# Behind the expert block: the projection of the delta gate goes last, and its Silu is taken straight from the projection's result

## The chip, the cores and the metric

The kernel runs on one core of one Trainium2 chip. Its time is the device time of one execution, in microseconds (us). Five engines work side by side, each in the order of its own program: TensorE (PE in the profile, with PEld for its weight loads), VectorE (DVE), ScalarE (ACT), GpSimd (POOL) and SyncE (SP), which here issues all the transfers. They wait for each other through semaphores.

## The reference, cut to what matters

Two blocks of a transformer follow each other over 256 tokens of width 1024. The first holds neighbourhood attention, a gated recurrence and 16 experts. The second begins with a hybrid mixer. Its input projection is one matrix, whose columns are cut into several parts:

```python
qkv = jax.nn.silu(depthwise_conv_centred(p[..., :OFF_Z_A], conv_w))          # 1536 columns
za = p[..., OFF_Z_A:OFF_BA_A].reshape(bsz, n_tok, A_HEADS, A_HEAD_DIM)       # 512 columns: "z"
ba = p[..., OFF_BA_A:OFF_Q_B]                                                # 16 columns
qb = rms_norm_2(p[..., OFF_Q_B:OFF_K_B].reshape(...), q_norm)                # 512 columns: "q"
kb = rms_norm_2(p[..., OFF_K_B:OFF_V_B].reshape(...), k_norm)                # 128 columns
vb = p[..., OFF_V_B:].reshape(bsz, n_tok, B_KV_HEADS, B_HEAD_DIM)            # 128 columns
...
y = rms_norm_2(o, out_norm) * jax.nn.silu(z.astype(F32))                     # delta_readout
```

The gated delta rule takes qkv and ba. Grouped-query attention takes qb, kb and vb, after an axial rotation of qb and kb. The gate z is wanted much later: it multiplies the delta rule's output when that is complete.

## The kernel before, in words

Everything is float32, and tokens lie in two tiles of 128 (t = 0, 1). Each engine has one long program, written out by hand. Loops on different engines meet only at semaphores, so the order in which a program is written is the order of work.

Weights pass through a ring of six slots in SBUF. SP issues the transfers in a fixed order, and each waits until the weights six places ahead in the order have been used. Matmul results go to eight PSUM banks, six of which rotate here. `bank_filled` says that a result is complete, `bank_drained` that it has been read.

The stretch behind the experts, in the order of TensorE's program:

- the twelve feature blocks of qkv ("qkv", line 1284), each passed through a short convolution on VectorE (L2415, L2419), a Silu on ScalarE (L3068) and a transpose on TensorE (L446, a helper that makes all 128x128 transposes);
- `project("hyb", "z", ...)` and then `project("hyb", "q", ...)`, 512 columns each for both token tiles. Their matmuls are recorded at L555;
- "bkv": the 16 columns of ba with grouped keys and values, 272 columns (L1308);
- transposes of the grouped queries ("qbT") once VectorE has given `grouped_query_ready`, and of the grouped keys ("kbT") once it has given `grouped_key_ready`. ScalarE copies them out (L3086, L3091);
- grouped attention: 16 steps (two token tiles, eight heads). A step has the scores (L1332), one eighth of a modulation product, which is independent work (L467), the transposes of the exponentials of two steps before (L446), and the product with the values of three steps before (L1345). The first three steps have scores and modulation only; then come the first transposes, the fourth step's scores and modulation, the second transposes, and with them the first values.

VectorE in the same stretch: it normalises the heads of qkv (L2176 to L2185), copies z out of PSUM (L2433), copies q out (L2438), takes q's mean squares, scales, rotates and scales again (L2444 to L2459, both tiles, which ends in `grouped_query_ready`), copies bkv out (L2463), and does the same for the keys (L2196 to L2475, which ends in `grouped_key_ready`). ScalarE takes the three square roots in it (L2690). The Silu of z runs on ScalarE behind the attention (L3100), in place, and `delta_gate` tells VectorE's readout of the delta rule, long after.

The first block's neighbourhood attention has the same form in its own lines: scores at L753 and L755, modulation at L467, transposes at L446, values at L768.

## Time and profile before

| | |
|---|---|
| time before, median of 3 runs | 2674.57 us (2674.56 to 2683.15) |
| span of the profiled execution | 2689.2 us |
| TensorE busy | 2163.9 us, 80% of the span |
| VectorE, ScalarE, GpSimd busy | 599.4, 343.5, 97.0 us |
| chain that ended last | TensorE 54%, transfers 40%, VectorE 3%, ScalarE 2% |

The profiled execution is one more execution of the same program, and the profile gives only its span. Line numbers (L555) are lines of the kernel before. A row of a timeline gives the start in us from the span's start, the time from the first to the last of the merged instructions, and what they are. In square brackets stands how long the engine was idle ahead of them and what released it. TensorE makes two records of one float32 matmul, so the counts in the trace are twice those of the program's order.

### The profile page before, as it was taken

To read this page: it belongs to the slowest core of one execution; us is meant where nothing else is said; L and a number is where in the kernel's file an instruction comes from. 1 tells how busy PE (TensorE), PEld (TensorE's weight loads), DVE (VectorE), ACT (ScalarE), POOL (GpSimd) and SP (SyncE) were. 2 spreads that over 40 slices of the span, in tenths; PEclk is the share of its full clock that TensorE was granted. 3 is DMA by queue.
4 is the path that set the end of the run, shared out by engine and by line. 5 is a ranking of instruction groups with operands and counts; after the bars stand their busy time and mean duration, and the time that the engine had idled before them with its cause. 6 is when DMAs were issued, how large, how long until landed. Compare 5 with 4: busy or idle time off the path is not lost.

```text
span 2689.2 us, 35584 instructions
## 1 busy us (share of the span) xinstructions
PE 2163.9 (80%) x15740; PEld 1251.1 (47%) x15740; DVE 599.4 (22%) x1143; ACT 343.5 (13%) x692; POOL 97.0 (4%) x116
## 2 busy tenths in 40 slices
PE   5999998555566565666988865587999999999999
PEld 2444574222223232233554432263576885666874
DVE  1112554001011010112322210055434000461000
ACT  2101222000010000011110100031251000132000
POOL 0001000000000000000111100000030000100000
PEclk8999998999999999999999999988899999999999
DMA  8633706999999999999999999953732454323450
GB/s 329 260 127 140 236 10 230 421 425 425 424 424 422 421 425 415 421 407 424 424 424 424 425 424 425 421 185 105 240 127 63 139 178 153 110 79 113 148 204 37
DMA packets 158907, 755.20 MB, mean 281 GB/s; under 512 B 12249, under 2 KB 75737, under 8 KB 102050
## 3 DMA queue, kind: packets, MB, share of 16 engines
q1 hardware_dynamic: 158754, 752.92, 70.6%
q8 instruction: 125, 2.05, 0.3%
q14 instruction: 28, 0.23, 0.0%
HBM read 751.83 MB, written 1.05 MB: 280 GB/s over the span
## 4 chain that ended last, share of the span: by engine, by line
PE 54%; DMA 40%; DVE 3%; ACT 2%; issue 1%; POOL 0%; DVEq 0%; SPq 0%; ACTq 0%; POOLq 0%
DMA ring<-w_up_dram 16%; PE psum L653 11%; DMA ring<-w_gate_dram 11%; DMA ring<-w_down_dram 8%; PE psum L555 8%; PE psum L681 5%; DMA ring<-hyb_w_dram 4%; PE psum L1176 3%; PE psum L467 2%; PE psum L1560 2%; PE psum L1240 2%; PE psum L446 2%; PE psum L1284 2%; PE psum L1382 1%; PE psum L1655 1%; PE psum L1015 1%
## 5 line engine op out<-in xcount | busy, mean ns | idle before, releaser
L1176 PE MATMUL psum<-ring,arena 128*32 128x320 f32 x4096 | 360.4, 469 | 281.0 <-DMA ring<-w_gate_dram 141.9
L1176 PEld LDWEIGHTS psum<-ring,arena 128*32 128x32 f32 x4096 | 112.0, 111 | 440.6 <-DMA ring<-w_up_dram 170.8
L653 PE MATMUL psum<-arena,ring 128*128 128x256 f32 x1408 | 305.5, 380 | 0.0
L1240 PE MATMUL psum<-ring,arena 128*32 128x512 f32 x1344 | 212.0, 606 | 107.3 <-DMA ring<-w_down_dram 107.3
L653 PEld LDWEIGHTS psum<-arena,ring 128*128 128x128 f32 x1408 | 268.5, 191 | 36.6
L555 PE MATMUL psum<-ring,arena 128*128 128x512 f32 x480 | 213.3, 606 | 10.3 <-ACT arena L2760 8.5
L1240 PEld LDWEIGHTS psum<-ring,arena 128*32 128x32 f32 x1344 | 47.4, 109 | 247.2 <-DMA ring<-w_down_dram 171.8
L555 PEld LDWEIGHTS psum<-ring,arena 128*128 128x128 f32 x480 | 92.7, 195 | 128.2 <-issue 128.2
L2337 DVE TENSOR_TENSOR arena<-arena,psum 128x320 f32<-128x320 f32 (+1 forms) x32 | 16.7, 521 | 580.5 <-PE psum L1176 574.6
L681 PE MATMUL psum<-ring,arena 128*128 128x512 f32 x288 | 125.0, 596 | 0.0
L1185 PE MATMUL psum<-ring,arena 128*32 128x64 f32 x2048 | 119.8, 291 | 0.0
L1185 PEld LDWEIGHTS psum<-ring,arena 128*32 128x32 f32 x2048 | 69.1, 111 | 84.1 <-issue 79.0
L446 PE MATMUL psum<-consts,arena 128*128 128x128 f32 x470 | 80.3, 309 | 30.8 <-DVE arena L1737 8.7
L467 PE MATMUL psum<-ring,cols 128*32 128x512 f32 x576 | 88.2, 717 | 18.1 <-DMA ring<-w_mod_dram 18.1
L446 PEld LDWEIGHTS psum<-consts,arena 128*128 128x128 f32 x470 | 62.9, 167 | 82.6 <-issue 54.0
L681 PEld LDWEIGHTS psum<-ring,arena 128*128 128x128 f32 x288 | 55.2, 192 | 68.6 <-issue 68.5
L1893 DVE TENSOR_TENSOR arena<-arena,psum 128x512 f32<-128x512 f32 x22 | 15.1, 687 | 290.3 <-PE psum L653 290.3
L1069 PE MATMUL psum<-arena 128*128 128x128 f32 x544 | 73.6, 284 | 1.3
L1069 PEld LDWEIGHTS psum<-arena 128*128 128x128 f32 x544 | 64.9, 193 | 16.6 <-issue 16.6
L3034 ACT COPY arena<-psum 128x512 f32<-128x512 f32 x32 | 18.8, 586 | 407.5 <-PE psum L1240 407.5
L3021 ACT ACTIVATE arena<-psum 128x320 f32<-128x320 f32 (+1 forms) x32 | 14.9, 465 | 376.7 <-PE psum L1176 372.7
L986 PE MATMUL psum<-arena 128*128 128x512 f32 x128 | 59.2, 605 | 0.8 <-issue 0.8
(376 smaller groups left out, 2121.0 us busy)
## 6 DMA issues: line engine op xcount, KB each, us to landing
ring<-w_gate_dram SPq DMA_DIRECT2D x128, 1376.0 KB, 18.1
ring<-w_up_dram SPq DMA_DIRECT2D x128, 1376.0 KB, 18.1
ring<-w_down_dram SPq DMA_DIRECT2D x112, 1536.0 KB, 19.9
ring<-w_mod_dram SPq DMA_DIRECT2D x72, 1024.0 KB, 5.1
ring<-w_ffn_in_dram SPq DMA_DIRECT2D x88, 512.0 KB, 5.1
ring<-w_ffn_out_dram SPq DMA_DIRECT2D x14, 1536.0 KB, 7.4
ring<-w_in_dram SPq DMA_DIRECT2D x16, 1024.0 KB, 5.6
ring<-hyb_w_dram SPq DMA_DIRECT2D x10, 1024.0 KB, 16.8
```

Of the source, the lines that this page charges most:

```text
L446: return nc.tensor.transpose(o, i, const("ident")[0:i.shape[0], 0:i.shape[0]])
L467: ins = nc.tensor.matmul(psum[32 * j:32 * j + 32, bank, :], stat, w[:, j, :], start=(k == 0), stop=(k == KT - 1), skip_group_check=True)
L555: ins = nc.tensor.matmul(banks[t][:, 0:n], XTt(kk, t), w[:, k, :], start=(kk == 0), stop=(kk == 7), skip_group_check=True)
L653: ins = nc.tensor.matmul(b[:, i * 256:(i + 1) * 256], ws[k // 4][:, k % 4, u, i * P:(i + 1) * P], R(XT + k * 256, 256), start=(k == 0), st ...
L681: ins = nc.tensor.matmul(banks[2 * t + c], R(HTF + k * 256 + t * P, P), w[:, (k % 3) * D + c * HALF:(k % 3) * D + (c + 1) * HALF], start=( ...
L986: ins = nc.tensor.matmul(b, R(SALL + e * 256 + t * P, P), R(YS + c * HALF, HALF), start=True, stop=True, skip_group_check=True)
L1069: ins = nc.tensor.matmul(result(tag)[:, h * P:(h + 1) * P], lhs(h), rhs(h), start=True, stop=True, skip_group_check=True)
L1176: ins = nc.tensor.matmul(banks[u][c][32 * j:32 * j + 32, 0:GMAIN], R(XST + k * HALF + e * CAP, CAP), w3[:, 64 * c:64 * c + 64, QGROUP * j: ...
L1185: ins = nc.tensor.matmul(banks[u][1][32 * j:32 * j + 32, GMAIN:GMAIN + GEXTRA], R(XST + k * HALF + e * CAP, CAP), extra, start=False, stop ...
L1240: ins = nc.tensor.matmul(ybanks[half][32 * c:32 * c + 32, :], stationary, w, start=((half, c) not in begun), stop=(unit >= 36), skip_group ...
L1284: ins = nc.tensor.matmul(b[:, 0:SEQ], w[:, k, f * P:(f + 1) * P], R(XT + k * 256, SEQ), start=(k == 0), stop=(k == 7), skip_group_check=True)
L1560: ins = nc.tensor.matmul(b[:, i * 256:(i + 1) * 256], ws[k // 4][:, k % 4, u, i * P:(i + 1) * P], R(XT + k * 256, 256), start=(k == 0), st ...
```

## The change

Grouped queries are projected first, then grouped keys and values, and the gate block z last. The three weight loads change places in the same way. VectorE no longer copies z out; ScalarE applies the Silu to z straight from PSUM, between its third square root and its copies of the transposed queries, with a load of the Silu table ahead of it. The two Silu instructions behind the attention and the semaphore `delta_gate` go, and the readout waits for the drained bank instead.

```diff
@@ TensorE
-            project("hyb", "z", range(2), 512)
             project("hyb", "q", range(2), 512)
             enlist(("hyb", "bkv"))
...
                     if t == 1 and k == 7:
                         frees(("hyb", "bkv"), ("bkv", t))
+            project("hyb", "z", range(2), 512)

             pe.wait_ge(grouped_query_ready, tally.due(grouped_query_ready, 2))
@@ VectorE
             unit_heads(tmp, [R(at + t * HALF, HALF) for at in (QL, KL) for t in range(TT)], 16, unit_qk_ready)
-            for t in range(TT):
-                v.wait_ge(bank_filled[bank_of(("hyb", "z", t))], nth(("hyb", "z", t)))
-                ins = v.tensor_copy(R(ZG + t * HALF, HALF), result(("hyb", "z", t)))
-                ins.then_inc(bank_drained[bank_of(("hyb", "z", t))], 1)
-                v.wait_ge(bank_drained[bank_of(("hyb", "z", t))], nth(("hyb", "z", t)))
...
             readout("dlo", [R(E0 + t * HALF, HALF) for t in range(TT)], row("out_norm"),
-                    lambda t: v.wait_ge(delta_gate, tally.due(delta_gate)),
+                    lambda t: v.wait_ge(bank_drained[bank_of(("hyb", "z", t))], nth(("hyb", "z", t))),
@@ ScalarE
             root(sm(592, 4))
+            a.preload_act_table(ACT.Silu)
+            for t in range(TT):
+                tag = ("hyb", "z", t)
+                a.wait_ge(bank_filled[bank_of(tag)], nth(tag))
+                ins = a.activation(R(ZG + t * HALF, HALF), result(tag), ACT.Silu)
+                ins.then_inc(bank_drained[bank_of(tag)], 1)
             for t in range(TT):
                 dst = R(QBT, 1024).rearrange("p (i n) -> p i n", i=4)[:, :, t * P:(t + 1) * P]
...
             betas(0)
-            for t in range(TT):
-                z = R(ZG + t * HALF, HALF)
-                a.activation(z, z, ACT.Silu).then_inc(delta_gate, 1)
-                a.wait_ge(delta_gate, tally.gave(delta_gate))
             gate_decays(0, "gsums", "gsums1")
@@ SyncE
-            proj_in("hyb", T["hyb_w"], 1536, 512, "z")
+            proj_in("hyb", T["hyb_w"], 2064, 512, "q")

             s.wait_ge(x_ready, tally.due(x_ready, 4))
             post_rows(T["g_mix_post"][0], T["g_ffn_post"][0], (WP2, WT2))
-            proj_in("hyb", T["hyb_w"], 2064, 512, "q")
             grouped_in(("hyb", "bkv"))
+            proj_in("hyb", T["hyb_w"], 1536, 512, "z")
```

The order of TensorE's instructions from the last feature block of qkv to the first scores, before: z and q are the first and the second half of the 32 matmuls at L555.

```order
L1284 MATMUL psum<-arena,ring 128x256 x8
L446 MATMUL psum<-consts,arena 128x128 x6
L555 MATMUL psum<-ring,arena 128x512 x32
L1308 MATMUL psum<-ring,arena 128x272 x16
L446 MATMUL psum<-consts,arena 128x128 x16
L1332 MATMUL psum<-arena 128x512
```

The same place in the changed kernel, whose lines lie one or two lower: q is the first row of 16 at L554, z the second.

```order
L1283 MATMUL psum<-arena,ring 128x256 x8
L445 MATMUL psum<-consts,arena 128x128 x6
L554 MATMUL psum<-ring,arena 128x512 x16
L1306 MATMUL psum<-ring,arena 128x272 x16
L554 MATMUL psum<-ring,arena 128x512 x16
L445 MATMUL psum<-consts,arena 128x128 x16
L1331 MATMUL psum<-arena 128x512
```

The 16 matmuls of z have moved from ahead of q to between bkv and the 16 transposes.

ScalarE's order from the last transposes of qkv to the first exponentials of the attention, before:

```order
L3077 COPY arena<-psum 128x2x128 x2
L2690 ACT_TABLE_LOAD
L2690 ACTIVATE small<-small 128x16 x2
L2690 ACTIVATE small<-small 128x4
L3086 COPY arena<-psum 128x4x128 x2
L3091 COPY arena<-psum 128x512 x2
L2956 ACT_TABLE_LOAD
```

And in the changed kernel, with the table load at L3077 and the Silu of z at L3081:

```order
L3071 COPY arena<-psum 128x2x128 x2
L2684 ACT_TABLE_LOAD
L2684 ACTIVATE small<-small 128x16 x2
L2684 ACTIVATE small<-small 128x4
L3077 ACT_TABLE_LOAD
L3081 ACTIVATE arena<-psum 128x512 x2
L3086 COPY arena<-psum 128x4x128 x2
L3091 COPY arena<-psum 128x512 x2
L2950 ACT_TABLE_LOAD
```

The load and the two Silu instructions now stand between the last square root and the first copy of transposed queries. The number of table loads in the program is the same, since the one ahead of the old Silu (L3100) is gone.

## Rows read from the trace of the kernel before

**Rows 1.** The page: its first line.

```profile
span 2689.2 us, 35584 instructions
```

**Rows 2.** TensorE's timeline from the projections to the first scores.

```profile
1823.43 27.63 PE L555 MATMUL psum<-ring,arena 128*128 128x512 f32 x64
1850.90 7.50 PE L1308 MATMUL psum<-ring,arena 128*128 128x272 f32 x32
1864.24 1.97 PE L446 MATMUL psum<-consts,arena 128*128 128x128 f32 x8 [5.85 <-DVE arena L2459]
1872.22 1.97 PE L446 MATMUL psum<-consts,arena 128*128 128x128 f32 x8 [6.01 <-DVE arena L2475]
1875.12 2.04 PE L1332 MATMUL psum<-arena 64*128 64x512 f32 x2 [0.93 <-ACT arena L3091]
```

**Rows 3.** VectorE's timeline of the same stretch.

```profile
1837.43 0.69 DVE L2433 COPY arena<-psum 128x512 f32<-128x512 f32 x1 [2.74 <-PE psum L555]
...
1851.17 0.69 DVE L2438 COPY arena<-psum 128x512 f32<-128x512 f32 x1 [2.74 <-PE psum L555]
...
1863.76 0.43 DVE L2459 TENSOR_SCALAR arena<-arena 128x512 f32<-128x512 f32 x1
...
1871.22 0.95 DVE L2475 COPY arena<-arena 128x256 f32<-128x256 f32 x3
```

**Rows 4.** ScalarE's timeline of the same stretch.

```profile
1866.73 0.20 ACT L2690 ACTIVATE small<-small 128x4 f32<-128x4 f32 x1 [11.46 <-DVE small L1721]
...
1874.28 0.59 ACT L3091 COPY arena<-psum 128x512 f32<-128x512 f32 x1 [0.27 <-PE psum L446]
...
1881.04 0.69 ACT L2776 ACTIVATE arena<-psum,small 128x512 f32<-128x512 f32 x1
```

**Rows 5.** ScalarE's groups in the feed-forward: Silu from PSUM (xcount, busy us, mean ns).

```profile
L2789 ACT ACTIVATE arena<-psum 128x512 f32<-128x512 f32 x11 | 6.6, 598 | 137.4 <-PE psum L653 137.4
```

**Rows 6.** Issues of hyb_w on SyncE's queue, and one's landing (KB, us).

```profile
1736.33 25.62 SPq L3406 DMA_DIRECT2D ring<-hyb_w_dram  x6
...
1786.56 23.04 SPq L3406 DMA_DIRECT2D ring<-hyb_w_dram  x4
...
ring<-hyb_w_dram SPq DMA_DIRECT2D x1, 1024.0 KB, 5.0
```

**Rows 7.** Chain that ended last, in the attention: start, us, what.

```profile
1881.03 1.86 PE psum L467 x8
...
1886.76 1.05 PE psum L446 x4
...
1896.34 0.84 PE psum L1345 x8
1897.17 1.05 PE psum L1332 x2
...
1900.65 1.05 PE psum L1332 x2
```

**Rows 8.** TensorE by stretches: us, busy, granted clock, share of DMA, GB/s.

```profile
262.80:265.00 2.20, 2.19 (x13) 0.94 0.03 7
265.00:278.40 13.40, 13.40 (x44) 0.50 0.70 235
...
1858.40:1862.00 3.60, 0.00 (x0) 1.00 0.74 228
1862.00:1875.10 13.10, 3.94 (x16) 0.51 0.04 18
1875.10:1892.50 17.40, 17.38 (x48) 0.50 0.54 182
```

**Rows 9.** TensorE's timeline into the first block's neighbourhood attention.

```profile
256.73 3.66 PE L446 MATMUL psum<-consts,arena 128*128 128x128 f32 x32
262.81 0.67 PE L753 MATMUL psum<-arena 64*128 64x256 f32 x2 [2.43 <-ACT arena L2843]
...
278.42 1.00 PE L768 MATMUL psum<-arena 128*128 128x64 f32 x8
```

**Rows 10.** VectorE's timeline behind the attention.

```profile
1943.84 1.29 DVE L1967 COPY arena<-psum 128x512 f32<-128x512 f32 x2 [3.95 <-PE psum L446]
```

More of the change, by code:

```diff
@@ L225, in program @@
         softplus_log = semaphore("softplus_log")
-        delta_gate = semaphore("delta_gate")
         conf_mean_in = semaphore("conf_mean_in")
```

## The prediction

> **What bounds the kernel now.** I began with the page's first line [rows 1], which gives the execution against which all sums are made, and went then to the stretch that the change touches, engine by engine. TensorE's timeline is the one to start with, since TensorE or what it waits for carries the end. The two projections run without a gap from 1823.43 and the keys' and values' projection follows them at once until 1850.90 + 7.50 = 1858.40 [rows 2]. Then TensorE stands still twice: 5.85 us for L2459, the last step of the grouped queries, and 6.01 us for L2475, the last step of the grouped keys. After a third wait of 0.93 us, for ScalarE's copies, the first scores start at 1875.12. Between the end of the projections and the first scores lie 16.72 us, with only 16 transposes in them.
>
> The reader should then look at VectorE, which both waits name. Its chain begins when the second tile of q is complete, with the copy at 1851.17, and goes on almost without idling to the end of the queries' work at 1863.76 + 0.43 = 1864.19 and of the keys' at 1871.22 + 0.95 = 1872.17 [rows 3]. So VectorE needs 13.0 us from that copy for the queries and 21.0 us for both. It was free long before: it waited 2.74 us for L555, that is for TensorE to finish q. What bounds this stretch is how early q is complete.
>
> The last view is the granted clock. It is 1.00 (2.4 GHz) until 1862, four microseconds into the first wait, and 0.50 (1.2 GHz) from there to the start of the values at about 1892.5, although TensorE is busy for 17.38 of the last 17.40 us [rows 8]. The wait is therefore paid a second time, in the first steps of the attention.
>
> **Part one: q ahead of z.** The amount of TensorE's work is the same, so the three projections end at 1858.40 as before. Now q comes first. The second copy of z, which stood at the end of the first projection, started at 1837.43 [rows 3]. The second copy of q starts there now. It stood at 1851.17, so VectorE's chain moves by 13.74 us. Nothing ahead of it holds it back, since VectorE waited 2.74 us for TensorE even there. The queries are ready at 1864.19 - 13.74 = 1850.45, and the keys at 1872.17 - 13.74 = 1858.43. The copies of bkv inside the chain, now at about 1850.5, find it complete at 1837.2 + 7.5 = 1844.7. The last square root, ScalarE's at 1866.73 [rows 4], comes at 1853.0, and it stands ahead of the Silu of z in ScalarE's order, so it does not wait for z.
>
> TensorE therefore comes out of z at 1858.40 and finds the queries ready since 8 us. The eight transposes of queries take about 0.9 us, since 32 such took 3.66 us at the full clock [rows 9], or 0.114 us each. The keys' turn comes at 1859.3, after their 1858.43. Both waits on VectorE go to nothing, with a margin of 8 us for the first and 0.9 us for the second. All 16 transposes end near 1860.2.
>
> **Part two: the Silu of z on ScalarE.** The operation itself, Silu from PSUM on 128x512, is in the trace at 598 ns [rows 5]. The first tile is complete at about 1855 and its Silu lies beside TensorE's work. The second is complete with TensorE's last z matmul, so it runs from about 1858.7 (the copies of rows 3 started 0.27 us behind the end of the matmuls) to 1859.3. Queued behind it are the four copies of queries and keys, for which the first scores wait. Their first input is complete at about 1859.1, so the Silu delays them by 0.2 us. Four copies of 0.59 us [rows 4] end at 1861.7, and 0.25 us later, as before (1875.12 behind 1874.28 + 0.59), the scores start, at 1861.9. The table load ahead of the Silu comes at about 1853.3, when ScalarE has nothing else to do until 1855. If that cover were gone it would cost its own length. Behind the attention, ScalarE loses two Silus and a load, but there VectorE waits 3.95 us for TensorE's transposes and not for ScalarE [rows 10], so I count nothing. The two copies of z that VectorE loses lay in its waits for TensorE, so they count nothing either.
>
> The sum of parts one and two is 1875.12 - 1861.9 = 13.2 us.
>
> **Part three: the weights.** In SyncE's order q takes z's place, so its transfers go out with the six issues from 1736.33, which are over by 1762, and it is wanted at 1823. The four issues from 1786.56 to 1809.6 were q's two and bkv's two; now they are bkv's two and z's two. With 5.0 us from issue to landing [rows 6] the last is in by 1815, and z is wanted at 1844.7. The modulation weights behind them wait for slots that come free at the same times as before, because the ring counts places and the sizes of work between are the same. Cost nothing, cover 30 us.
>
> **Part four: the clock.** The attention's steps are priced at both levels by rows 7. At 0.50 the modulation takes 1.86 us and four transposes 1.05; at 1.00 the scores take 1.05 and a whole step from one L1332 to the next 1900.65 - 1897.17 = 3.48. Before, everything ahead of the values ran at 0.50: 17.4 us. What it does now is the one thing that this trace does not show for this place, so I bound it. At the lower end the clock is at half for the whole of it, and nothing is gained. At the upper end it stays at full: scores and modulation take 1.05 + 1.86 / 2 = 2.0 us a step, three steps end at 1867.9, and the transposes then wait for ScalarE's first exponential. That started 1881.04 - 1874.87 = 6.17 us behind the last key copy and took 0.69 [rows 4], so it now ends near 1868.6. TensorE starts 0.25 us later, and with transposes at half of 1.05, another step and transposes again (0.5 + 2.0 + 0.5) the values start at 1871.9, where before they started at 1892.5. That is a gain of 20.6 us in all, 7.4 of them from the clock.
>
> Between the two ends there is a near relative of this place in the same trace. The neighbourhood attention also comes behind dense projections and a train of transposes, then waits 2.43 us for ScalarE's copies, and starts with scores on 64 rows and modulation [rows 9]. The wait here will be 1.7 us. There the clock was 0.94 in the mean over the first 2.2 us and then 0.50 for 13.4 us, in which TensorE was busy all the time, and full again as the values began [rows 8]. Its way from first scores to first values was 278.42 - 262.81 = 15.6 us, against 17.4 us here. I take that value, the nearest row: 1.8 us gained, to be added to 13.2, so 15.0 us.
>
> The Trainium skill, in "TensorE: Matmul & The Clock Gate", Part 1, says that "activity releases the throttle", so that a busy array has the full clock again soon. By that rule the half clock of a busy stretch would be short, and the sum would be the upper end. Rows 8 speak against it, with 13.4 us and 17.4 us at 0.50 and full busy time. Part 4 of the same page says that transposes don't count as TensorE's work in the same way; with the projections' end as the last real work, that would favour the fall that rows 8 and 9 show.
>
> **The rivals.** *The clock stays up* (chance 0.27): the wait is shorter than in the relative, 1.7 against 2.43 us, and transposes end closer to it. The values then start at 1871.9, the gain is 20.6 us and the time 2654.0 us. Against it stands the relative, which fell.
>
> *The clock comes back late* (0.16): the clock is half from the first scores on, as before, and comes back not with the first values but some 3 us into them. Each microsecond at half does half the work, so this costs 1.6 us of the 13.2. The gain is 11.6 us and the time 2663.0 us. For it speaks that the two returns seen came within half a microsecond of the first values and need not again; against it, that it happened twice.
>
> *The waits only move* (0.05): if ScalarE's queue or the keys' chain is later than I think, the scores wait again. The margin of the keys is 0.9 us, every microsecond beyond it costs one, and 12 us would have to be found to bring the gain near nothing. I see no such row. The time would be 2672 us or so.
>
> *It becomes slower* (0.04): the attention is entered at half clock and stays there. A step at half takes twice the scores, 1.86 us of modulation, 1.05 of transposes and twice 0.84 of values, together 6.7 us against 3.48 [rows 7], 3.2 us more. Beyond 13.2 / 3.2 = four such steps with values in them the change loses, and eight and a half cost another 0.5%. Against it: in both attentions the clock came back with the first values.
>
> **How the numbers follow.** My forecast (0.48) is 15.0 us less. Against the profiled span that is 2689.2 - 15.0 = 2674.2 us. The median of the runs lies 14.6 us under that span; the stretch I changed waits for no transfer, so I take the same difference from the median: 2674.6 - 15.0 = 2659.6 us. With the next two cases the sum of chances is 0.91, from 2654.0 to 2663.0, and I give 3 us on both sides for runs that differ and for where clock changes fall behind the attention: 2651 to 2666. Half a per cent, 13.4 us, is about what a measurement of this kernel can tell from no change, and lies only 1.6 us below the forecast, so I let a quarter of the first case fall short of it: faster is three quarters of 0.48, the 0.27 of the second case and a little of the third, 0.66; slower 0.04; the rest, 0.30, is the same.
>
> **What would show it.** Right: TensorE goes from z into transposes with no wait for VectorE. The wait ahead of the first scores is under 2 us, for ScalarE's key copies. The first scores come 13 us earlier against the start of the projections (38.5 us behind it instead of 51.7). The first values come 53 to 55 us behind the start of the projections if the clock falls, 49 if it holds, and 69 before. Wrong: a wait for VectorE ahead of the keys' transposes of more than 1 us, a wait for hyb_w at the z projection, or a granted clock at half in the steps with values.

## The result

Five executions of the changed kernel have a median of 2652.93 us (2646.3 to 2668.32); five of the kernel before, on the same chip and in the same call, 2683.15 us (2674.56 to 2696.42). The ratio is 0.9894 [0.9862, 0.9926], so the change makes the kernel 1.1% faster. A second measurement of the same code gave 0.9886 [0.9866, 0.9905]. The 72 executions of the kernel before that ran beside the other kernels have a mean of 2686.0 us, the 11 of the changed kernel one of 2657.3 us: 28.7 us less, give or take about 4.5. (The 2674.57 us of the first table, a median of three, lies 11.4 us below that mean.) Left out of means and ratios are two executions of the kernel before at over 3000 us and one of `filler`, further down, at 2720.61 us.

TensorE's timeline of the changed kernel, from the last transposes of qkv into the attention, in the columns of [rows 2]. Lines lie one or two lower than before.

```profile
1813.69 0.44 PE L445 MATMUL psum<-consts,arena 128*128 128x128 f32 x2 [2.15 <-ACT arena L3062]
1813.97 15.60 PE L554 MATMUL psum<-ring,arena 128*128 128x512 f32 x32
1829.40 7.50 PE L1306 MATMUL psum<-ring,arena 128*128 128x272 f32 x32
1836.73 13.90 PE L554 MATMUL psum<-ring,arena 128*128 128x512 f32 x32
1850.47 1.91 PE L445 MATMUL psum<-consts,arena 128*128 128x128 f32 x16
1853.85 1.09 PE L1331 MATMUL psum<-arena 64*128 64x512 f32 x2 [1.47 <-ACT arena L3091]
1854.87 1.06 PE L466 MATMUL psum<-ring,cols 128*32 128x512 f32 x8
...
1860.60 0.66 PE L445 MATMUL psum<-consts,arena 128*128 128x128 f32 x4 [0.57 <-ACT arena L2770]
...
1863.73 1.00 PE L1344 MATMUL psum<-arena 128*128 128x64 f32 x8
```

The two waits for VectorE of [rows 2] are gone, and all 16 transposes are one group of 1.91 us. Scores take 1.09 us and modulation 1.06 us from the first step on; in the kernel before they took 2.04 and 1.86. The first scores start 39.88 us behind the projections' start (51.69 before), the first values 49.76 us behind it (69.08 before).

VectorE's timeline of the changed kernel, which answers to [rows 3]:

```profile
1829.67 0.69 DVE L2432 COPY arena<-psum 128x512 f32<-128x512 f32 x1 [2.74 <-PE psum L554]
...
1842.27 0.43 DVE L2453 TENSOR_SCALAR arena<-arena 128x512 f32<-128x512 f32 x1
...
1849.72 0.95 DVE L2469 COPY arena<-arena 128x256 f32<-128x256 f32 x3
```

ScalarE's timeline of the changed kernel, which answers to [rows 4]:

```profile
1845.23 0.20 ACT L2684 ACTIVATE small<-small 128x4 f32<-128x4 f32 x1 [11.46 <-DVE small L1720]
1845.46 1.28 ACT L3077 ACT_TABLE_LOAD   x1
1847.23 0.60 ACT L3081 ACTIVATE arena<-psum 128x512 f32<-128x512 f32 x1 [0.49 <-PE psum L554]
1850.67 0.60 ACT L3081 ACTIVATE arena<-psum 128x512 f32<-128x512 f32 x1 [2.84 <-PE psum L554]
1851.16 1.20 ACT L3086 COPY arena<-psum 128x512 f32<-128x512 f32 x2
1852.39 1.20 ACT L3091 COPY arena<-psum 128x512 f32<-128x512 f32 x2
...
1859.77 0.69 ACT L2770 ACTIVATE arena<-psum,small 128x512 f32<-128x512 f32 x1
```

The keys are ready at 1849.72 + 0.95 = 1850.67, the queries 8 us before, and TensorE goes from z into the transposes at 1850.47. What TensorE still waits for is ScalarE's four copies.

TensorE by stretches in the changed kernel, with the columns of [rows 8] (behind PE's busy time those of PEld, DVE, ACT and POOL, then the granted clock):

```profile
1813.00:1829.00 16.00, 15.30 (x34) 6.77 (x35) 9.70 (x17) 2.66 (x5) 0.00 (x0) 0.89 0.28 101
1829.00:1850.00 21.00, 21.00 (x65) 12.13 (x64) 18.15 (x43) 2.30 (x4) 0.00 (x0) 1.00 0.44 150
1850.00:1862.00 12.00, 9.96 (x54) 3.88 (x52) 4.71 (x15) 9.27 (x16) 0.00 (x0) 1.00 0.69 237
1862.00:1875.00 13.00, 13.00 (x87) 6.93 (x86) 5.48 (x9) 3.06 (x9) 0.00 (x0) 1.00 0.96 352
```

The clock is 1.00, so 2.4 GHz, from the transposes through the first steps of the attention, where [rows 8] have 0.50. It is below 1.00 only at the start of the projections, behind the 2.15 us wait: 0.89 over 16 us, which is some 3.5 us at half. Therefore q took 15.60 us and not 13.9.

**Where the time went.** Five marks on TensorE's timeline divide an execution: A, the first matmul of qkv (L1283 or L1284); B, the start of the projections; C, the first scores; D, the first values; E, the first sum of the gates behind the attention (L1053 or L1054); F, the first matmul of the next feed-forward (L652 or L653). All in us, from one profiled execution each.

| profile | A at | B to C | C to D | D to E | A to E | E to F | F to end | span |
|---|---|---|---|---|---|---|---|---|
| before | 1775.19 | 51.69 | 17.39 | 46.42 | 163.74 | 139.28 | 611.0 | 2689.2 |
| before_again | 1776.63 | 51.71 | 17.39 | 46.58 | 164.27 | 145.49 | 608.4 | 2694.8 |
| after | 1765.87 | 39.88 | 9.88 | 46.23 | 144.09 | 135.30 | 605.8 | 2651.1 |
| after_again | 1766.05 | 38.19 | 9.88 | 46.24 | 142.63 | 133.53 | 610.6 | 2652.8 |

In the changed stretch, A to E, the two pairs differ by 164.0 - 143.4 = 20.6 us. The profiled executions differ by 40 us, because those of before also came to A 10.0 us later, and took 9.5 us longer from E on. Ahead of A the change only has another block of hyb_w loaded, and behind E only the Silu of z is gone (two of 0.63 us and a load). Behind that Silu ScalarE still waited 1.03 us for TensorE in the kernel before, so it was not in the way. Of the 28.7 us between the many executions this stretch accounts for 20.6 us, and some 8 us are to be sought elsewhere.

### The profile page after: what moved, and what is told of

Its sections match the earlier page's. It is cut to its first block and busy times, and to the rows that moved or that the text cites. A ratio compares the mean times of both kernels' runs of the same rounds, so it can differ in the third digit from the quotient of the medians.

```text
span 2651.1 us, 35579 instructions
## 1 busy us (share of the span) xinstructions
PE 2132.5 (80%) x15740; PEld 1235.2 (47%) x15740; DVE 598.3 (23%) x1141; ACT 343.1 (13%) x692; POOL 97.3 (4%) x116
## 5 line engine op out<-in xcount | busy, mean ns | idle before, releaser
L652 PE MATMUL psum<-arena,ring 128*128 128x256 f32 x1408 | 306.4, 381 | 0.0
L652 PEld LDWEIGHTS psum<-arena,ring 128*128 128x128 f32 x1408 | 269.1, 191 | 36.9
L554 PE MATMUL psum<-ring,arena 128*128 128x512 f32 x480 | 215.6, 610 | 10.4 <-ACT arena L2754 8.6
L554 PEld LDWEIGHTS psum<-ring,arena 128*128 128x128 f32 x480 | 93.5, 196 | 129.6 <-issue 129.5
L2336 DVE TENSOR_TENSOR arena<-arena,psum 128x320 f32<-128x320 f32 (+1 forms) x32 | 16.7, 521 | 580.6 <-PE psum L1175 574.6
L466 PE MATMUL psum<-ring,cols 128*32 128x512 f32 x576 | 79.9, 656 | 18.3 <-DMA ring<-w_mod_dram 18.3
L445 PE MATMUL psum<-consts,arena 128*128 128x128 f32 x470 | 74.9, 293 | 19.2 <-DVE arena L1736 8.3
## 6 DMA issues: line engine op xcount, KB each, us to landing
ring<-hyb_w_dram SPq DMA_DIRECT2D x10, 1024.0 KB, 16.7
```

What stands on the lines that cost most here:

```text
L445: return nc.tensor.transpose(o, i, const("ident")[0:i.shape[0], 0:i.shape[0]])
L466: ins = nc.tensor.matmul(psum[32 * j:32 * j + 32, bank, :], stat, w[:, j, :], start=(k == 0), stop=(k == KT - 1), skip_group_check=True)
L554: ins = nc.tensor.matmul(banks[t][:, 0:n], XTt(kk, t), w[:, k, :], start=(kk == 0), stop=(kk == 7), skip_group_check=True)
L652: ins = nc.tensor.matmul(b[:, i * 256:(i + 1) * 256], ws[k // 4][:, k % 4, u, i * P:(i + 1) * P], R(XT + k * 256, 256), start=(k == 0), st ...
```

## The experiments

My theory behind the first result was that two effects add up: the chain on VectorE starts earlier, some 13 us, and TensorE's waits ahead of the attention no longer cost it the clock, 7.4 us. The rivals were that the Silu's place has a part in it, that the clock falls or holds by the position in time and not by the waits, and that the gain beyond 20.6 us belongs to the new order too. Twelve kernels ran: two repeat the two kernels, three do or undo one part, five put idle or busy time at one place, and two go beyond the change. Each ratio is to the kernel before on the same chip.

### The two kernels again

`after_again` and `before_again` are the two kernels without an edit.

> The changed kernel once more, with a profile of its own, to part what the change does from what differs between executions. In the first profiles the span fell by 38.1 us, of which 19.3 lie between the start of the projections (1823.43 before, 1813.97 after) and the end of the attention, 9.5 ahead of it and 9.3 behind it. Theory: only the 19 us belong to the change; the other 19 are chance, so this profile's stretch from the end of the attention to the end of the span lies anywhere between the two seen (750.3 and 741.0 us), and the ratio is near 0.993 (19 of 2680). Rival: the change also shortens what follows, then the stretch behind the attention is again 741 us within 2 and the ratio near 0.989.

Measured: 2658.2 us, ratio 0.9886 [0.9866, 0.9905]. Here the clock did not fall at the start of q:

```profile
1814.10 0.44 PE L445 MATMUL psum<-consts,arena 128*128 128x128 f32 x2 [2.15 <-ACT arena L3062]
1814.37 13.90 PE L554 MATMUL psum<-ring,arena 128*128 128x512 f32 x32
...
1852.56 1.09 PE L1331 MATMUL psum<-arena 64*128 64x512 f32 x2 [1.47 <-ACT arena L3091]
```

q takes 13.90 us, and the first scores come 38.19 us behind the projections' start. The 1.7 us by which the first profile was later are the half clock at the start of q, and nothing else. Before the run I had taken only 19 us for the change's own, with a ratio near 0.993; the rival there, that the gain goes on behind the attention, asked for a ratio near 0.989 and for 741 us from E to the end within 2. The ratio came as the rival had it, and the stretch from E on took 744.1 us, between the two. So 0.9894 was not a chance of the first measurement.

> The kernel before once more, for a second profile. The first block, which no variant touches, took 9.4 us longer up to the feature blocks of qkv in the two profiles with z first (before, and the Silu alone) than in the four with q first, and the difference lies in the neighbourhood attention, where the clock fell in the two and not in the four. Theory: that is chance, decided by some tenths of a microsecond of where TensorE stands when the clock is reviewed, so it may come out either way here; the stretch from the projections to the end of the attention is 115.5 us again. Rival (something in the changed program keeps the clock up in the first block): the feature blocks start at 1775 again. Ratio 1.000.

Measured: 2686.2 us, ratio 1.000 [0.9975, 1.0026]. A difference under 0.3% is not to be told from none. A came at 1776.63, and the clock fell in the first block's attention again: the sign that I had named for the rival, that something in the changed program keeps the clock up there. Later runs speak against its plain form, since that clock also fell in `gap12` and `covered_one_table`, which have the new order, and held in `filler6`, which has the old one.

### The order alone, and the Silu alone

`order_only` has the changed order on TensorE and SyncE. VectorE copies z behind the keys, and ScalarE does the Silu behind the attention as before. Against the changed kernel:

```diff
@@ VectorE, ahead of log_decays(0)
+            for t in range(TT):
+                v.wait_ge(bank_filled[bank_of(("hyb", "z", t))], nth(("hyb", "z", t)))
+                ins = v.tensor_copy(R(ZG + t * HALF, HALF), result(("hyb", "z", t)))
...
@@ ScalarE
-            a.preload_act_table(ACT.Silu)
-            for t in range(TT):
...
-                ins = a.activation(R(ZG + t * HALF, HALF), result(tag), ACT.Silu)
...
             betas(0)
+            for t in range(TT):
+                z = R(ZG + t * HALF, HALF)
+                a.activation(z, z, ACT.Silu).then_inc(delta_gate, 1)
```

> The three projections and their weights in the changed order, but the gate handled as before: VectorE copies z out (now behind the keys, ahead of the log decays), ScalarE takes the Silu behind the attention. Theory (the order is the cause): no wait of TensorE for VectorE ahead of the transposes, the first scores about 39 us behind the start of the projections, as in the changed kernel (39.9). The two z copies of 0.69 us then stand ahead of the soft plus and so of the first exponential, which comes 1 to 1.5 us later; the time is within 3 us of the changed kernel's. Rival (the gain lies in taking the Silu at once): the time is near that of before.

Measured: 2663.8 us, ratio 0.9903 [0.9879, 0.9927]. The median is 5.6 us above that of `after_again`, measured beside it, where I had expected 3 at most, but the intervals overlap. The first exponential did not come later either: it starts 5.92 us behind the first scores in both. In the stretch it is the same within 0.02 us: B to C 39.90 and C to D 9.88. The order carries the gain of the stretch.

`silu_only` keeps z first and gives ScalarE the Silu from PSUM, with a load of the square root's table behind it. VectorE's two copies and the Silu behind the attention go, as in the changed kernel:

```diff
@@ ScalarE, against the kernel before
             root(sm(576, 16))
+            a.preload_act_table(ACT.Silu)
+            for t in range(TT):
+                tag = ("hyb", "z", t)
+                a.wait_ge(bank_filled[bank_of(tag)], nth(tag))
+                ins = a.activation(R(ZG + t * HALF, HALF), result(tag), ACT.Silu)
+                ins.then_inc(bank_drained[bank_of(tag)], 1)
+            a.preload_act_table(ACT.Sqrt)
             root(sm(576, 16))
             root(sm(592, 4))
```

> The projections and weights in the order of before (z, q, keys and values), but ScalarE takes the Silu of z straight from PSUM, between its first square root and the second, with loads of the Silu and the square-root table around it; VectorE's two copies and the Silu behind the attention are gone. Theory: nothing on the path changes, TensorE waits 5.9 and 6.0 us for VectorE as before, the first scores come 51.7 us behind the start of the projections, and the ratio is 1.000 within the noise. Rival (the Silu is the gain): most of the 19 us between the projections and the attention's end appear here.

Measured: 2683.5 us, ratio 0.9987 [0.9963, 1.001]. TensorE's waits stand as in [rows 2]:

```profile
1864.49 1.97 PE L445 MATMUL psum<-consts,arena 128*128 128x128 f32 x8 [5.79 <-DVE arena L2453]
1872.48 1.97 PE L445 MATMUL psum<-consts,arena 128*128 128x128 f32 x8 [6.02 <-DVE arena L2469]
```

Where the Silu stands is worth nothing by itself. In the changed kernel it only must not be in the way of the copies, and it is not: with it the scores come 1853.85 - 1850.47 = 3.38 us behind the start of the transposes, in order_only, without it, 1853.77 - 1850.37 = 3.40.

### Keys and values last

`bkv_last` has the order q, z, bkv on TensorE and SyncE:

```diff
@@ TensorE and SyncE, against the changed kernel
             project("hyb", "q", range(2), 512)
+            project("hyb", "z", range(2), 512)
             enlist(("hyb", "bkv"))
...
-            project("hyb", "z", range(2), 512)
```

> As the changed kernel, but z between q and the keys' and values' projection, which comes last. Theory: the queries' work is hidden, the keys' is not, since VectorE can only begin it with bkv complete. TensorE waits about 7.4 us for VectorE ahead of the keys' transposes (8.0 us of key work behind the end of the projections, less the queries' transposes), and the first scores come near 46 us behind the start of the projections instead of 39.9. Whether the clock falls in that wait is open: 6 us slower than the changed kernel if it holds, 13 if it falls. Rival (it is enough that q comes first): no wait there, and the changed kernel's time.

Measured: 2678.9 us, ratio 0.9967 [0.9948, 0.9986].

```profile
1850.47 1.04 PE L445 MATMUL psum<-consts,arena 128*128 128x128 f32 x8
1858.28 1.97 PE L445 MATMUL psum<-consts,arena 128*128 128x128 f32 x8 [6.77 <-DVE arena L2469]
1861.21 2.04 PE L1331 MATMUL psum<-arena 64*128 64x512 f32 x2 [0.96 <-ACT arena L3091]
```

The same kernel by stretches, from the last 1.9 us of that wait to the values:

```profile
1856.40:1878.60 22.20, 19.36 (x56) 5.99 (x57) 6.50 (x19) 7.87 (x14) 0.00 (x0) 0.50 0.42 142
```

The queries are ready as in the changed kernel, the keys are not: one wait of 6.77 us stays. From its last 1.9 us on the clock is half for 22 us, and C to D takes 17.39 us as before. So one of the two waits was enough to lose the clock. The median is 20.7 us above that of `after_again`, where I had expected 13; 16 of these lie in A to E.

### Busy work in the waits, in the old order

`filler` and `filler6` are the kernel before with matmuls whose result nobody reads, 12 (6) ahead of each of the two waits for VectorE:

```diff
@@ TensorE, against the kernel before
+            for i in range(6):
+                nc.tensor.matmul(psum[:, 6, :], const("ident"), R(XT, HALF), start=True, stop=True, skip_group_check=True)
             pe.wait_ge(grouped_query_ready, tally.due(grouped_query_ready, 2))
```

> The kernel before, with 12 idle matmuls (128x128 by 512 columns, results never read) in each of the two waits for VectorE, so that TensorE works through both at its full clock. 12 of 0.43 us fill 5.2 of 5.9 and of 6.0 us. Theory (the second half of the gain is the clock): the first scores come 51.7 us behind the start of the projections as before, but the first values about 10 us behind the first scores instead of 17.4, and the whole is 7.5 us faster than before. Rival (the half clock belongs to the attention's first steps, whatever comes ahead): 17.4 us again and the time of before, or worse.

Measured: 2675.3 us, ratio 0.9966 [0.994, 0.9991]. I had sized the filling wrongly: such a matmul takes 0.87 us, so 12 of them took 10.46 us and pushed the scores back by 6.7 us. Still the clock held and C to D took 9.89 us. In the stretch 6.7 us were lost and 7.5 won, so the ratio's 9 us are for the most part not from there.

> The kernel before with six more 128x128x512 matmuls, whose results nobody reads, in each of TensorE's two waits for VectorE (5.85 and 6.01 us); everything else as before. By the trace of the first such kernel one of these takes 0.87 us, so six take 5.2 us and fit into each wait. If idleness of TensorE ahead of the attention is what brings the clock down: the first scores come at 51.7 us behind the start of the projections as before, the clock stays at full, and the first values come some 10 us behind the scores instead of 17.4, at 61.6. That would be 7.4 us in the stretch, and a ratio of 0.995 to 0.998 to the kernel before. If transposes are what lets the clock go, whatever stands in the waits: values at 69 as before, ratio 1.000.

Measured: 2673.8 us, ratio 0.9949 [0.9931, 0.9967].

```profile
1852.86 5.31 PE L1316 MATMUL psum<-arena,consts 128*128 128x512 f32 x12
1858.88 1.09 PE L446 MATMUL psum<-consts,arena 128*128 128x128 f32 x8 [0.70 <-DVE arena L2463]
1859.80 5.32 PE L1323 MATMUL psum<-arena,consts 128*128 128x512 f32 x12
1866.86 1.09 PE L446 MATMUL psum<-consts,arena 128*128 128x128 f32 x8 [1.74 <-DVE arena L2479]
1869.06 1.09 PE L1336 MATMUL psum<-arena 64*128 64x512 f32 x2 [1.11 <-ACT arena L3095]
```

And by stretches, over the first steps of the attention:

```profile
1869.00:1879.00 10.00, 9.36 (x49) 2.77 (x50) 4.16 (x9) 6.45 (x11) 0.00 (x0) 1.00 0.68 229
```

Here the chain on VectorE is as late as in the kernel before, and the scores start 51.00 us behind B. But the clock is 1.00 over the first steps, and the values come 9.89 us behind the scores and not 17.39. So it was TensorE's idleness that took the clock, and the two effects stand apart: of the 20.6 us some 13 were the late chain and 7.5 the clock. The second part can be had in the old order too, with work that computes nothing: A to E takes 155.32 us, 8.7 less than the mean of the two profiles of before.

### Idle time ahead of the scores, in the new order

`gap2` and `gap12` are the changed kernel with 2 (12) more copies on ScalarE ahead of the key copies, for which TensorE waits. They change no result.

```diff
@@ ScalarE, against the changed kernel
+            for i in range(2):
+                a.copy(diagonals[:, :], consts[:, 0:TT * P]).then_inc(scalar_done, 1)
+                a.wait_ge(scalar_done, tally.gave(scalar_done))
             for g in range(2):
                 a.wait_ge(bank_filled[bank_of(("kbT", g))], nth(("kbT", g)))
```

> The changed kernel with two idle copies (128x256, about 0.37 us each) on ScalarE between its copies of the queries and of the keys, so that TensorE waits about 2.2 us ahead of the first scores instead of 1.5. That is the wait of the first block's attention (2.4 us), from which I forecast a fall of the clock. If the clock falls there: first values about 56 us behind the start of the projections, 6 us slower than the changed kernel. If it holds: 50.5 us and 0.7 us slower.

Measured: 2665.2 us, ratio 0.9919 [0.989, 0.9949].

```profile
1851.65 1.09 PE L1331 MATMUL psum<-arena 64*128 64x512 f32 x2 [2.34 <-ACT arena L3094]
1852.67 1.91 PE L466 MATMUL psum<-ring,cols 128*32 128x512 f32 x8
```

By stretches, from the first scores on:

```profile
1851.60:1855.00 3.40, 3.35 (x11) 0.96 (x12) 0.28 (x2) 2.81 (x4) 0.00 (x0) 0.67 0.03 10
1855.00:1865.50 10.50, 10.50 (x36) 2.35 (x36) 3.88 (x8) 3.62 (x7) 0.00 (x0) 0.62 0.81 263
```

In this one profile a wait of 2.34 us instead of 1.47 goes with just the picture that I had forecast for the changed kernel: the first scores run at full clock, the modulation behind them at half, and C to D takes 14.07 us, 4.2 more for 0.87 us of wait.

> As the last, with twelve such copies: a wait of about 6 us. Theory: the clock falls in it, as in the waits of before, and comes back with the values: first scores 44.5 us behind the start of the projections, first values 62, and 12 us slower than the changed kernel, where the wait alone is 4.5. Rival (only the length of the wait counts): 4.5 us slower.

Measured: 2674.6 us, ratio 0.996 [0.994, 0.9979].

```profile
1866.64 2.04 PE L1331 MATMUL psum<-arena 64*128 64x512 f32 x2 [6.71 <-ACT arena L3094]
```

```profile
1866.60:1879.30 12.70, 12.65 (x35) 2.93 (x36) 2.78 (x7) 5.65 (x9) 0.00 (x0) 0.51 0.50 166
```

With 6.71 us the clock is half from the first scores on, and C to D takes 15.08 us. The wait itself is 5.2 us longer than in the changed kernel and the clock adds as much again. The first values come 58.50 us behind B and not 62, since in this profile q ran at full clock and the clock was back one step ahead of the values.

### Two more matmuls ahead of the transposes

`shift2` puts two matmuls that nobody reads behind z, so that the scores start later without any idleness.

```diff
@@ TensorE, against the changed kernel
             project("hyb", "z", range(2), 512)
+            for i in range(2):
+                nc.tensor.matmul(psum[:, 6, :], const("ident"), R(XT, HALF), start=True, stop=True, skip_group_check=True)
```

> The changed kernel with two more 128x128x512 matmuls, whose results nobody reads, between the projection of z and the transposes: 1.74 us of busy TensorE, no idleness. First scores about 41.6 us behind the start of the projections (38.2 to 39.9 in the two profiles of the changed kernel, plus 1.74), first values 9.9 us behind the scores. If the theory holds that it is the order (TensorE's idleness ahead of the scores) that keeps the clock, not the tenth of a microsecond at which the scores start, the clock stays at full here too. If the position decides, it falls at the scores and the values come 13 to 17 us behind them. From the attention's end to the feed-forward part some 135 us if the 10.2 us of half clock there belong to the old order, 140 if they belong to a position.

Measured: 2666.1 us, ratio 0.9918 [0.9893, 0.9944]. B to C 41.54 us, C to D 9.89: the clock held at this position too. From E to F 135.98 us, which by my expectation meant that the half clock there belongs to the old order. The rows say otherwise. The first two rows are TensorE behind E in this kernel, by stretches, and then the same in the kernel before:

```profile
1917.00:1929.00 12.00, 11.11 (x122) 10.55 (x123) 5.69 (x9) 2.67 (x5) 2.10 (x2) 0.57 0.01 2
```

```profile
1938.90:1950.90 12.00, 11.10 (x124) 10.54 (x125) 6.05 (x9) 4.78 (x8) 2.10 (x2) 0.57 0.00 1
```

and in the changed kernel:

```profile
1909.90:1921.90 12.00, 9.80 (x198) 8.98 (x199) 7.79 (x12) 3.41 (x6) 3.30 (x3) 1.00 0.01 2
```

Half clock behind the attention, 0.57 in the mean of 12 us, is thus not a matter of the old order. It comes in the new order as well, with the attention's start 1.7 us further from B.

### Beyond the change

`covered` takes up what the first profile showed, the waits of 0.75 and 2.15 us ahead of q. The first half of q goes ahead of the last two groups of transposes, which wait for ScalarE.

```diff
@@ TensorE, against the changed kernel
-            for ff in (10, 11):
-                pe.wait_ge(short_conv_ready, tally.due(short_conv_ready))
-                transpose4(("qkvT", ff), [R(COUT + ff % 2 * HALF + t * P, P) for t in range(TT)])
-            project("hyb", "q", range(2), 512)
+            def last_transposes():
+                for ff in (10, 11):
+                    pe.wait_ge(short_conv_ready, tally.due(short_conv_ready))
+                    transpose4(("qkvT", ff), [R(COUT + ff % 2 * HALF + t * P, P) for t in range(TT)])
+            project("hyb", "q", range(2), 512, last_transposes)
```

> The changed kernel with the first half of the q projection ahead of the last two transposes of qkv, for which TensorE waits 0.75 and 2.15 us on ScalarE in the changed kernel; the second half stands behind them. If that wait is on the path, the way from the first qkv matmul to the first scores, 88.0 us in the changed kernel's profile, shortens by 2.9 us to 85.1; if the waiting is also what dropped the clock 1.4 us behind the start of q, by up to 1.6 us more, to 83.5. Ratio to the kernel before some 0.988. If VectorE's chain is held by something else ahead (log decays, its own backlog), nothing: 88.0.

Measured: 2657.6 us, ratio 0.9889 [0.9865, 0.9913].

```profile
1810.96 7.03 PE L554 MATMUL psum<-ring,arena 128*128 128x512 f32 x16
1817.83 0.60 PE L445 MATMUL psum<-consts,arena 128*128 128x128 f32 x4
1818.26 7.03 PE L554 MATMUL psum<-ring,arena 128*128 128x512 f32 x16
...
1849.58 1.09 PE L1334 MATMUL psum<-arena 64*128 64x512 f32 x2 [1.47 <-ACT arena L3094]
```

Both waits are gone and q runs at full clock. From A to C it takes 44.28 + 38.62 = 82.90 us, where the changed kernel took 87.98 and, at full clock, 86.51. The theory of the path was right, 0.6 us more than it asked for. Yet the median is that of the changed kernel: A to E is 3.6 and 5.1 us shorter than in the two profiles of the changed kernel, at most 0.2% of 2657, and the interval is 0.5% wide.

`covered_one_table` adds a named table set with both Exp and Ln ahead of the softplus, and puts the first part of the modulation ahead of the first scores.

```diff
@@ ScalarE and TensorE, against covered
+            a.preload_act_table_set("natural_log_exp_and_others")
             softplus(0)
             attention("gq", WP2)
...
+            modulation_part("mod2_1", 0, 0, 4)
...
-            attention("gq", 16, scores2, values2, lambda i: modulation_part("mod2_1", i // KT, i % KT, 4 + i // KT))
+            attention("gq", 16, scores2, values2,
+                      lambda i: i < 15 and modulation_part("mod2_1", (i + 1) // KT, (i + 1) % KT, 4 + (i + 1) // KT))
```

> As the kernel before it in this list, and two more edits ahead of the attention: ScalarE's softplus (Exp, then Ln) takes the one table set that has both functions, named by hand, so that one load of 1.28 us stands there instead of three; and the first part of the modulation goes ahead of the first scores, into TensorE's wait of 1.5 us for ScalarE's copies. If the loads are on ScalarE's path to the first exponential: it starts 2.6 us earlier against the first scores' release, and TensorE's wait for it behind the scores (0.57 us in the changed kernel) goes; with the modulation part (0.93 us) moved into the wait, the way from the first qkv matmul to the first values is 1.5 us shorter than in the kernel before it in this list. If not, under 0.5 us.

Measured: 2655.6 us, ratio 0.9881 [0.9852, 0.9909]. ScalarE's timeline, with one load where three stood:

```profile
1856.36 1.21 ACT L3096 COPY arena<-psum 128x512 f32<-128x512 f32 x2
1857.59 1.28 ACT L3098 ACT_TABLE_LOAD   x1
1858.88 0.22 ACT L2955 ACTIVATE small<-small 128x16 f32<-128x16 f32 x1
1859.47 0.21 ACT L2958 ACTIVATE small<-small 128x16 f32<-128x16 f32 x1 [0.37 <-DVE small L2230]
1861.19 0.69 ACT L2775 ACTIVATE arena<-psum,small 128x512 f32<-128x512 f32 x1 [1.50 <-DVE small L1854]
```

The first exponential starts 1861.19 - 1857.82 = 3.37 us behind the first scores, in the changed kernel 1859.77 - 1853.85 = 5.92: 2.55 us earlier, as expected. It now waits 1.50 us for VectorE's row maxima (L1854). For TensorE that was worth its wait of 0.57 us, which is gone. The values come at 44.43 + 47.86 = 92.29 us behind A, in covered at 92.80: 0.5 us earlier and not 1.5. The rest comes at the end of the attention, which lacks the moved part: A to E is 137.52 against 139.03 us. It has the shortest stretch and the lowest median of the twelve experiments, but no interval parts it from the changed kernel.

The Trainium skill says in "ScalarE: Activation LUTs", section "Table sets: the hidden batching unit", that one set holds exp and ln, so that both cost one load. The trace agrees. The page gives about 2.7 us for a load, the drain included; here each load instruction took 1.28 us.

## Why the prediction came out as it did

The forecast was 2659.6 us and 15.0 us of gain, with a range of 2651 to 2666; the median was 2652.9 us. The time lay in the range and the direction was right. The case that I called the likeliest is not what happened. What happened is the first rival, "the clock stays up", to which I gave 0.27.

That the time fell into the range is in part luck. The forecast stood on a base of 2674.6 us, a median of three executions, and the mean of 72 is 2686.0, 11.4 us more. In gain I was off by almost a factor of two: 15.0 us were forecast, and 28.7 us lie between the means, 30.2 between the medians. That mean less 15.0 us would have been 2671.0 us, above the range. The rival's 2654.0 us is as lucky: its gain of 20.6 us is the stretch's, 8.1 us short of the whole, and the low base hides that.

**Part one, q ahead of z, was right.** VectorE's chain was to move by 13.74 us against the projections. The second copy of q stood 1851.17 - 1823.43 = 27.74 us behind B and now stands 1829.67 - 1813.97 = 15.70 us behind it, 12.04 us less, and the difference of 1.7 us is the half clock at the start of q, which the repetition did not have. Both waits for VectorE vanished, the keys' with a margin of 0.7 us where 0.9 was worked out (ready at 1850.67, wanted 0.9 us behind 1850.47). First scores 38.5 us behind B were forecast; 39.88 and 38.19 were measured. The sum of parts one and two, 13.2 us, came out at 11.8 and 13.5.

**Part two, the Silu, was right.** It was to cost 0.2 us and cost 0.0 (3.38 us from the first transposes to the scores, against 3.40 in order_only). The wait left over for ScalarE was to be 1.7 us and was 1.47. silu_only shows the other half, that moving the Silu alone brings nothing to be measured.

**Part three, the weights, was right.** No wait for hyb_w stands at any projection of the changed kernel. SyncE's timeline has its last four issues done at 1777.11 + 22.41 = 1799.5. The five such transfers of 1024 KB issued between 1700 and 1830 took 5.5 us in the median from issue to landing, where 5.0 was assumed from one. Even with the 16.7 us of all ten in the program z is there at 1816, and it is wanted at 1836.73:

```profile
1726.74 25.90 SPq L3402 DMA_DIRECT2D ring<-hyb_w_dram  x6
...
1777.11 22.41 SPq L3402 DMA_DIRECT2D ring<-hyb_w_dram  x4
```

**Part four, the clock, is the step that failed.** I wrote: "I take that value, the nearest row: 1.8 us gained", from the first block's attention, where the clock fell behind a wait of 2.43 us. The bound that I had set beside it, values 49 us behind B if the clock holds, was measured at 49.76 and 48.07, and C to D at 9.88 us where 1871.9 - 1861.9 = 10.0 was worked out. With the full clock the stretch's gain was to be 20.6 us; it was 19.65 and 21.1 (A to E, 163.74 - 144.09, and 163.74 - 142.63). So the rival's gain in the stretch was sized to within a microsecond, and it was ranked wrongly.

Two things were wrong with the nearest row. First, the wait there was longer, 2.43 us against 1.7 forecast and 1.47 measured. Behind waits of 1.42 to 1.49 us the clock held in five of five profiles, and in gap2, with 0.87 us more, it fell. That is what one would see if the length of the wait decides, but it is not shown: gap2 is one profile. Second, I took one execution of the relative for its behaviour. All 14 profiles of this study have the same code there and the same wait of 2.39 to 2.43 us. The rows are TensorE's timeline into that attention in the changed kernel, as in [rows 9]:

```profile
263.38 0.67 PE L752 MATMUL psum<-arena 64*128 64x256 f32 x2 [2.40 <-ACT arena L2837]
...
272.64 1.00 PE L767 MATMUL psum<-arena 128*128 128x64 f32 x8
```

Here the clock held, and the values come 9.26 us behind the scores, not 15.61. Of the 14 profiles eight have 9.3 us, five have 15.6 and one has 17.2. The row that I used was one of two outcomes of a wait of 2.4 us, and the rarer one. With that known, the upper end would have been the better forecast.

**What the sum lacked.** The stretch gives 20.6 us and the executions differ by 28.7, give or take 4.5. Two things could fill the rest, and neither is settled. The start: up to A, the profiles of before are 9.1 to 10.8 us later than those of the changed kernel. In the first block's attention the clock costs 6.3 us in one of them and 8.0 in the other. With the new order A came at 1763 to 1767 in order_only, bkv_last, gap2 and covered, and at 1775 in gap12 and covered_one_table, in which the clock fell there; in shift2 it did not fall there, and A came at 1772. If that is chance alone, it cancels in the mean. But it fell in four of the five profiles with the old order and in two of the nine with the new, so that it is chance alone is not shown either.

Behind the attention: E to F takes 139.28, 145.49 and 135.31 us in the three profiles whose waits stand as before (the third is silu_only), mean 140.0, and 129.3 to 139.7, mean 134.7, in the other eleven. These some 5 us have the right size. The traces show what they are: the granted clock, in the mean from E to F, was 0.92, 0.88 and 0.95 in the three profiles and 0.94 to 0.99 in the eleven, and over all 14 the stretch is in the main the longer the lower that mean is (129.29, 132.25 and 134.03 us at 0.99, 145.49 at 0.88). It is not only the fall at E. shift2 and silu_only have that one too, with 135.98 and 135.31 us; before_again has another, 0.85 in the mean of the 69 us that begin 60 us behind E. And over the eleven kernels with an edit, the gain by the ratio less the gain in A to E is between -0.3 and +7.9 us, with a mean of 5. So something of about 5 us comes with nearly every edit. The Silu at E is not it: order_only keeps it there and has 135.10 us. Why the clock falls more often behind the attention in the kernel before, and whether the starts differ in the mean, stays open. No run here parts them.

**The rules of the chip.** The Trainium skill says in "TensorE: Matmul & The Clock Gate", Part 1, that activity releases the throttle. By that rule alone I would have taken the upper end, the 20.6 us that the stretch gave. Rows 8 spoke against the rule and still do: in gap12 TensorE is busy for 12.65 of 12.70 us at 0.51, in bkv_last 19.36 of 22.20 us at 0.50. What decided here was not how soon the clock comes back but that it did not fall ahead of the scores, and the same part says that idleness lets it fall. The runs agree with that: with the waits filled it held, in the old order too.

## What to carry to other kernels

A wait on TensorE can have two prices, its own length and the half clock behind it, and here the second was 7.5 us behind 12 us of waits; so read the granted clock in the stretch behind each wait, and ask of an edit not only how much it shortens the wait but also what the clock does behind what is left of it. A clock effect seen once in a trace is one draw: look for the same code in all profiles at hand before it is taken as the rule of the place. When independent projections follow one another, the one whose result has the longest way through the other engines goes first, and all whose results are waited for go ahead of the one that nobody waits for; getting one of two right (q, z, bkv) brought 9 us where both brought 29.

## What the runs showed of the hardware that I had not expected

- The same instructions behind the same wait of 2.4 us ran at full clock in 8 of 14 profiles and at half in 6. It held where the scores started at 263.29 to 264.05 us, and fell at 261.89 to 263.15, but also once at 263.51, while it held in gap2 at 263.50. The position goes with the outcome but does not settle it.
- A busy TensorE stayed at 1.2 GHz for 12 to 17 us in the first steps of the attention (busy 12.65 of 12.70 us at 0.51 in gap12, 17.38 of 17.40 at 0.50 in the kernel before). In the grouped attention it was back at 2.4 GHz before the first values or less than 2 us behind them, in every profile in which it had fallen.
- The clock fell at the start of the dense q projection, behind a wait of 2.15 us, in the profiles of the changed kernel, order_only, bkv_last, gap2 and shift2, and not in those of after_again and gap12. It cost 1.7 us. With z first it did not fall in five profiles, with the wait covered in none of two. Why it falls there only with q first is not known.
- A 128x128x512 matmul of the filling took 0.87 us at full clock, as two records in the trace; I had counted 0.43. A 128x128 transpose made one record only; 16 of them took 1.91 us, 0.12 each.
